# Casting a tile's weights one piece per matmul group instead of eight pieces per unit, in a hybrid decoder layer on Trainium2

## The reference

```python
u = rms_norm(h, norm_mix_g)
z_pool, z_q, z_k, z_v, z_gp, z_ga = split(u @ w_in)
pooled = multiscale_pool(z_pool)                    # windows 2/4/8/16, minus the token
mixed = einsum("blgc,gcd->blgd", pooled, pool_w)
y_pool = (mixed * pool_scale) @ w_pool_br
y_attn = sliding_window_attention(q, k, v, sinks, rel_bias) @ w_attn_br
merged = sigmoid(z_gp) * y_pool + sigmoid(z_ga) * y_attn
h = h + merged @ w_out
u2 = rms_norm(h, norm_mlp_g)
h = h + square(relu(u2 @ w_up)) @ w_down
h = rms_norm(h, norm_final_g)
```

## Time and profile before

| | us |
|---|---|
| median of 2 runs | 2581.69 (2487.75 and 2675.64) |
| the profiled execution | 2486.95 |
| its span on the slowest core, core 6 | 2485.4 |
| spans of the 8 cores | 2475.5 to 2485.4 |

### The profile page before, as it was taken

How to read it: one execution, slowest core, us unless ns; L and a number is a source line. 1 busy time by engine, 2 the same in 40 slices (tenths; PEclk the granted TensorE clock), 3 DMA queues, 4 the chain that set the end, 5 groups by cost and what they waited for, 6 DMA issues and landing times.

```text
span 2485.4 us, 28994 instructions; the slowest of 8 cores (2475.5 to 2485.4 us)
## 1 busy us (share of the span) xinstructions
PE 2139.6 (86%) x10254; PEld 976.0 (39%) x10432; DVE 607.6 (24%) x958; ACT 963.0 (39%) x1390; POOL 266.0 (11%) x262
## 2 busy tenths in 40 slices
PE   0575787698899989998799979998799988999798
PEld 0242233353444434443344524443344534444343
DVE  0112410224302250124302251024402242023401
ACT  5345554355212643155321543146321643124431
POOL 0000022000230004000040003100050002200050
PEclk9887998899999999999999999999999999999999
DMA  6876388741236303442145413453134502443132
GB/s 204 264 269 231 136 281 265 257 170 68 102 141 220 140 34 135 151 181 102 68 157 192 151 38 132 153 191 122 68 136 161 202 35 102 170 161 136 61 126 86
DMA packets 48990, 372.74 MB, mean 150 GB/s; under 512 B 5568, under 2 KB 5568, under 8 KB 32336
## 3 DMA queue, kind: packets, MB, share of 16 engines
q1 hardware_dynamic: 48848, 370.87, 42.1%
HBM read 321.04 MB, written 49.81 MB: 149 GB/s over the span
## 4 chain that ended last, share of the span: by engine, by line
PE 67%; DMA 11%; ACT 11%; issue 5%; DVE 4%; SPq 2%; ACTq 0%; DVEq 0%
PE ps L356 46%; PE ps L654 16%; ACT PT L529 4%; DMA stg<-w_dn 3%; DMA stg<-w_up 2%; PE ps L551 2%; DVE PT L531 2%; PE ps L553 1%; ACT tmpf L561 1%; SPq L259 1%; ACT sqj L316 1%; ACT wring L276 1%; PE ps L332 1%; DVE PT L534 1%; DMA stg<-w_q 1%
## 5 line engine op out<-in xcount | busy, mean ns | idle before, releaser
L637 POOL TENSOR_TENSOR arena<-tmpf 128x512 bf16<-128x512 f32 x256 | 265.2, 1041 | 2154.4 <-ACT tmpf L635 2154.3
L654 PE MATMUL ps<-wring,arena 128*128 128x512 bf16 x2008 | 444.4, 381 | 14.1 <-ACT tmpf L635 8.8
L356 PE MATMUL ps<-uT,wring 128*128 128x512 bf16 x1812 | 410.5, 385 | 19.4 <-ACT tmpf L635 11.6
L356 PE MATMUL ps<-Emp,wring 128*128 128x512 bf16 x1812 | 407.8, 384 | 8.1 <-DVE Emp L338 6.0
L654 PEld LDWEIGHTS ps<-wring,arena 128*128 128x128 bf16 x2048 | 201.0, 98 | 256.3 <-issue 16.9
L356 PEld LDWEIGHTS ps<-uT,wring 128*128 128x128 bf16 x1856 | 183.1, 99 | 238.7 <-issue 30.5
L356 PEld LDWEIGHTS ps<-Emp,wring 128*128 128x128 bf16 x1856 | 182.6, 99 | 225.3 <-issue 15.4
L635 ACT ACTIVATE tmpf<-ps 128x512 f32<-128x512 f32 x256 | 152.4, 597 | 299.4 <-PE ps L356 269.6
L529 ACT ACTIVATE PT<-ps 128x1536 bf16<-128x1536 f32 x128 | 184.7, 1443 | 154.4 <-PE ps L524 151.6
L356 PE MATMUL ps<-arena,wring 128*128 128x512 bf16 x616 | 144.4, 394 | 25.0 <-DVE arena L565 21.3
L553 PE MATMUL ps<-PT,cb 128*64 128x512 bf16 x384 | 145.2, 378 | 0.0
(11 more groups left out here) (82 smaller groups left out, 1775.0 us busy)
## 6 DMA issues: line engine op xcount, KB each, us to landing
wring<-w_up_bf SPq DMA_DIRECT2D x28, 2048.0 KB, 7.9
wring<-w_dn_bf SPq DMA_DIRECT2D x28, 2048.0 KB, 7.9
stg<-w_up SPq DMA_DIRECT2D x32, 512.0 KB, 7.3
stg<-w_dn SPq DMA_DIRECT2D x32, 512.0 KB, 8.3
wring<-w_pool_bf SPq DMA_DIRECT2D x7, 2048.0 KB, 7.8
wring<-w_q_bf SPq DMA_DIRECT2D x7, 2048.0 KB, 8.6
wring<-w_gp_bf SPq DMA_DIRECT2D x7, 2048.0 KB, 11.6
wring<-w_ga_bf SPq DMA_DIRECT2D x7, 2048.0 KB, 7.8
```

The lines of the kernel that those rows point to most:

```text
L356: ins = e.matmul(o, lhsT=pairs[kc][0], rhs=pairs[kc][1], start=(kc == 0), stop=(kc == nk - 1))
L637: P.op("pool", lambda e, c=c, ti=ti: e.tensor_tensor(out=arena[:, c, :], in0=tmpf[:, ti, :], in1=tmpf[:, ti, :], op=ALU.mult), reads=[("tm ...
L654: ins = e.matmul(bank(bk), lhsT=arena[:, j * 8 + kc, b * 128:(b + 1) * 128], rhs=w[:, kc, half * 512:(half + 1) * 512], start=(j == 0 and ...
```

## The change

The first tile's casts are no longer put into the queues all at once. `issue_unit` appends loads, casts and the store to lists. `pump()` takes the next cast (and a store that stands ahead of it) off the list and is called once ahead of each matmul group; `flush_upto(n)`, called by `need`, forces out whatever of unit n is left. `emit_loads()` keeps up to four loads ahead of the casts that have been taken off, across the border between units. The casts are also dealt out differently: two of three to ScalarE instead of three of four. Tiles 1 to 7 are written as before.

```diff
+    WQ = {"loads": [], "ops": [], "li": 0, "ci": 0, "groups_done": 0, "ngroups": 0}
...
+    def emit_loads():
+        while WQ["li"] < len(WQ["loads"]) and WQ["li"] < WQ["groups_done"] + NSTG:
+            WQ["loads"][WQ["li"]]()
+            WQ["li"] += 1
+
+    def pump_one():
+        n_, fn, closes, kind = WQ["ops"][WQ["ci"]]
+        WQ["ci"] += 1
+        fn()
+        if closes:
+            WQ["groups_done"] += 1
+        emit_loads()
+        return kind
+
+    def pump():
+        while WQ["ci"] < len(WQ["ops"]):
+            if pump_one() == "cast":
+                break
+
+    def flush_upto(n):
+        while WQ["ci"] < len(WQ["ops"]) and WQ["ops"][WQ["ci"]][0] <= n:
+            pump_one()
...
-                P.dma("sp", f"stg{s}",
+                WQ["loads"].append(lambda s=s, u=u, p=p, npc=npc, pc=pc: P.dma(
...
-                    eng = ("act", "act", "dve", "act")[cast_rr[0] % 4]
+                    eng = ("act", "dve", "act")[cast_rr[0] % 3]
...
-                    P.op(eng, fn, reads=[("stg", s), "scl"], writes=[("ws", slot, piece)])
+                    WQ["ops"].append((n, lambda eng=eng, fn=fn, s=s, slot=slot, piece=piece: P.op(
+                        eng, fn, reads=[("stg", s), "scl"], writes=[("ws", slot, piece)]), q == npc - 1, "cast"))
...
             W["issued"] += 1
+        flush_upto(n)
...
     def mm_group(b, nk, lhs_fn, rhs_fn, reads, out=None):
+        pump()
```

More of the change, by code:

```diff
@@ L237, in build_program @@
         si = (si + 1) % NSTG
-    stg_i = [si]
     W = {"issued": 0}
     cast_rr = [0]
+    WQ = {"loads": [], "ops": [], "li": 0, "ci": 0, "groups_done": 0, "ngroups": 0}
     def wslot_keys(slot):
         return [("ws", slot, p) for p in range(8)]
+    def emit_loads():
[17 more added lines that the diff above has]
+            pump_one()
     def issue_unit(n):
@@ L255, in issue_unit @@
                 npc = min(per_load, 8 - p)
-                s = stg_i[0]
-                stg_i[0] = (s + 1) % NSTG
-                P.dma("sp", f"stg{s}",
-                      lambda e, s=s, u=u, p=p, npc=npc, pc=pc: e.dma_start(out=stg[:, s, 0:npc * pc],
-                                                                           in_=wsrc[u][:, p * pc:(p + npc) * pc]),
-                      writes=[("stg", s)])
+                s = WQ["ngroups"] % NSTG
+                WQ["ngroups"] += 1
+                WQ["loads"].append(lambda s=s, u=u, p=p, npc=npc, pc=pc: P.dma(
+                    "sp", f"stg{s}",
+                    lambda e: e.dma_start(out=stg[:, s, 0:npc * pc], in_=wsrc[u][:, p * pc:(p + npc) * pc]),
+                    writes=[("stg", s)]))
                 for q in range(npc):
@@ L279, in issue_unit @@
                                                                                     scalar2=None, op0=ALU.mult)
-                    P.op(eng, fn, reads=[("stg", s), "scl"], writes=[("ws", slot, piece)])
+                    WQ["ops"].append((n, lambda eng=eng, fn=fn, s=s, slot=slot, piece=piece: P.op(
+                        eng, fn, reads=[("stg", s), "scl"], writes=[("ws", slot, piece)]), q == npc - 1, "cast"))
                 p += npc
             if nt > 1:
-                P.dma("sp", f"wst{u}", lambda e, u=u, slot=slot, sz=sz: e.dma_start(out=wbf[u], in_=wring[:, slot, 0:sz]),
-                      reads=wslot_keys(slot), writes=[("wbf", u)])
+                WQ["ops"].append((n, lambda u=u, slot=slot, sz=sz: P.dma(
+                    "sp", f"wst{u}", lambda e: e.dma_start(out=wbf[u], in_=wring[:, slot, 0:sz]),
+                    reads=wslot_keys(slot), writes=[("wbf", u)]), False, "store"))
+            emit_loads()
         else:
@@ L645, in build_program @@
                 assert W["issued"] >= NU
+                flush_upto(NU - 1)
                 load_x(1)
```

## The result

| | before | changed |
|---|---|---|
| median of all executions, us | 2488.87 (8) | 2459.45 (9) |
| ratio to before, with its 95% interval | | 0.9887 (0.9874 to 0.9900) |
| profiled execution, us | 2486.95 | 2459.09 |
| its span, us | 2485.4 | 2457.5 |
| spans of the 8 cores, us | 2475.5 to 2485.4 | 2443.3 to 2457.5 |

The change is 1.1% faster. The forecast was 2455 us, 1.3% less than before.

The account below looks back on a forecast made before the run. The first tile was taken to be bound by the weights' arrival, paced by the DMA queue. 31 + 8.3 - 8 = 31 us off 2486.95 us gave 2455 us, with a range from 2420 to 2488.

Parts of the forecast that it names:

- the forecast's own case: The forecast is for executions like the lower of the two runs shown before the change, 2487.75 us.
- (a): First tile, unit borders: closing the transfer holes at each unit's end wins 2.4 us at 13 borders, 31 us.
- (b): Ahead of attention: the last w_pb groups run while w_out is still coming in, which removes 8.3 us.
- (c): Behind attention and the RMSNorm: casts standing behind bank evictions add 3 us and 5 us, together 8 us.
- (d): End of the first tile: w_dn3's matmuls start at the last unit's store in both kernels, counted as nothing.
- rival C: First tile: TensorE working in small bites keeps the lower clock, 0.50, so the kernel is slower, 2534 us; chance 0.05.
- A: First tile: with the queue never empty, transfers run at 334 GB/s, 19 us per unit, giving 2425 us; chance 0.18.
- B: First tile: the rate is shared and other cores already use the holes; stays at 269 GB/s, 2487 us; chance 0.12.
- D: First tile: loads go out early, but casts behind evictions free their buffers no sooner, giving 2491 us; chance 0.07.
- T(8) near 206 and T(16) near 418: First tile: the stores of units 8 and 16 are issued near 206 us and near 418 us.
- windows below 200 GB/s at borders: First tile: no 4 us window at a unit border should be below 200 GB/s, except at w_pb.

Follow-up runs that it names:

- three of four: The changed kernel, but with three of four casts on ScalarE as before, instead of two of three: 2465.24 us, ratio to before 0.9900.
- ahead plus w_out: The kernel with only the loads ahead of the stores, with the w_out casts alone interleaved as well: 2454.34 us, ratio to before 0.9879.
- from w_up3 on: The kernel with loads ahead and w_out interleaved, with the casts of w_up3 and all w_dn units interleaved too: 2450.60 us, ratio to before 0.9870.

## Why the prediction was right

Its place, its mechanism and its sum hold: 2459.45 us against 2455, in the forecast's own case. Several terms are off with opposite signs, though, and that the sum is so close is in part luck. The terms, from the averages over 8 cores:

| term | forecast, us | measured, us | from |
|---|---|---|---|
| (a) holes before attention, 7 borders | -16.8 | -17.8 | T(8), before to changed |
| (b) the tail | -8.3 | -7.6 | item 1 behind T(8): 7.2 to -0.4 |
| (c) behind attention | +3 | +4.9 | item 1 to T(9): 55.9 to 60.8 |
| (a) w_up0 to w_up1 | -2.4 | -3.3 | T(9) to T(10): 23.0 to 19.7 |
| (c) behind the norm | +5 | +7.0 | T(10) to T(11): 23.8 to 30.8 |
| (a) five borders after it | -12 | -13.1 | T(11) to T(16): 115.8 to 102.7 |
| sum to T(16) | -31.5 | -29.9 | T(16): 445.9 to 416.0 |
| (d) end of the tile | 0 | +2.1 | T(16) to first output store: 8.3 to 10.4 |
| (d) later tiles | 0 | -2.9 | first output store to the end: 2025.4 to 2022.5 |
| whole sum | -31.5 | -30.7 | mean of the 8 spans: 2479.6 to 2448.9 |

(a) was worked out as 2.4 us per border from the bytes missing in a 4 us hole, and came out at 2.5 before attention and 2.6 after the norm. It wasn't that each hole closed: the 2 us up to a store carry 226 GB/s on the average, and 121 in the window shown. The rate behind it rose too: 353 GB/s in the ten microseconds from 384 on, beside 326 before. The experiment with only the loads ahead shows that this term alone carries the change: ratio 0.9894 without any interleaving.

(b) is confirmed twice, by putting it back (7.2 us at item 1) and by taking it alone (item 1 from 6.7 us behind T(8) to 0.3).

(c) was under-sized at both places, 4.9 for 3 and 7.0 for 5. I had worked out the eighth cast from the pace of the matmul groups, and it came later. (a) was under-sized by 3.0 us, so that the two errors nearly cancel in the table. The prediction put the whole interleaving at 8.3 - 8, near nothing, and for the whole kernel so it is: with the loads ahead in both, adding it changes the ratio from 0.9894 to 0.9887, within the intervals. But this too is a sum of opposite parts. At T(16) the kernel with only the loads ahead is 2.5 us sooner than the change (413.5 and 416.0), and its later tiles take 2.8 us longer (2025.3 and 2022.5). Without the loads ahead the interleaving costs 0.4%.

(d), nothing at the end of the tile, did not hold. Before, w_dn3's last matmul came 14.3 us behind T(16) on the average, in the change 16.4. The w_dn3 row of core 4, before and changed:

```profile
444.04 13.97 PE L654 MATMUL ps<-wring,arena 128*128 128x512 bf16 x64 [1.78 <-ACT wring L270]
410.42 16.73 PE L684 MATMUL ps<-wring,arena 128*128 128x512 bf16 x64 [7.41 <-ACT wring L293]
```

TensorE now waits 7.41 us for the last cast, and the first 4 us of the stage run at the lower clock:

```profile
444.04:448.04 4.00, 4.00 (x19) 1.85 (x20) 0.90 (x2) 0.00 (x0) 0.00 (x0) 1.00 0.94 385
410.42:414.42 4.00, 4.00 (x10) 1.43 (x11) 0.26 (x1) 0.00 (x0) 0.00 (x0) 0.50 0.94 328
```

It does 10 matmuls in them instead of 19. This comes near rival C's mechanism, for a part of one stage.

The later tiles, which I had expected to take the same time, take 2.9 us less, and the record shows with what this goes along. In the five traces of kernels with three of four casts on ScalarE (before, loads ahead only, three of four, ahead plus w_out, and from w_up3 on) the stretch from the first output store to the end takes 2025.3 to 2027.5 us. In the seven traces with two of three it takes 2021.3 to 2022.9, also where both kinds ran on one chip. The casts themselves are over by then, and the tiles are written alike; why they differ stays open. (The trace of the first run with only the loads ahead, of a 2821.44 us execution, is not counted.)

The rivals. A (334 GB/s, 2425 us) fell: with the DMA engines busy 95% of the time the rate is 304 GB/s, so little is left to gain with this mix of loads and stores. Its premise was also read too narrowly. The 334 GB/s of rows 9 are the best 10 us of the first tile, not of the trace; in a later tile the kernel before reaches more, and the changed kernel has 392 GB/s from 430 to 440 us. So the prediction's remark that the best 10 us stay below the figure that it cites does not hold. Core 6, before:

```profile
500.00:510.00 10.00, 9.95 (x47) 4.51 (x46) 0.69 (x1) 2.98 (x5) 0.00 (x0) 1.00 0.90 360
```

A's 23 us after attention should also have been 449.6 - 423 = 26.6, which changes nothing here.

B (holes already used by other cores) fell: the windows of all 8 cores show 301 to 309 GB/s from 62 to 200 us where they showed 263 to 274, so that closing all cores' holes raised all rates. C fell as a whole with the clock of 0.97 from 312 to 410 us; it was 0.88 on core 6 in the same window before. In small it is real: in w_dn3, and in attention once casts were put there (clock 0.83). D fell at T(8), though its observation is right that interleaved casts free the staging buffers later. That this keeps the rest of the holes open is argued from the order of the queues, not tried.

Of the signs I had named, T(8) near 206 and T(16) near 418 came out at 206.1 and 425.3 on the slowest core, 202.4 and 416.0 over all of them. The full units from w_up3 on take 20.5 us, not 21.7, and T(11) comes 30.8 us behind T(10), not 28. One sign failed: windows below 200 GB/s at borders are still there (170 at 379 to 383 us). It was a poor sign, since the kernel with the interleaving alone shows 167 and 151 in such windows with its holes open.

## What to carry to other kernels

Where a store waits in the same in-order DMA queue as the next loads, put those loads ahead of it as far as staging buffers come free. The hole between them is worth its missing bytes at the rate beside it, and here that gave 31.2 us for 34.2 measured. Interleaving casts with the work that empties banks paid in these traces only where that work was otherwise held up in the chain that ends last (here ahead of attention, and 1.7 us at w_dn); where data already waits in staging, it should be taken in one go. A moment inside the kernel that comes sooner is not yet time won: follow it to the first output store and to the end, since here 9.6 us at T(16) became 2.3 us of the mean span.

## What I had not expected of the hardware

Eight casts added to attention (about 8 us together) made that stretch 7.6 us longer on the average of the cores, and 10 on core 0 (45.4 to 55.5 us), though ScalarE was busy for only about two thirds of it. Idle time inside a chain of small hand-offs was not free: at a clock of 0.97 the casts still cost 6.2 to 6.4 us. The rest goes along with a lower granted clock, down to 0.83, in a stretch where it had been 1.00 on all cores.

The windows of 2 us up to a unit's store carry 6 and 16 GB/s in the two kernels whose loads stand behind the store, and 226 and 259 in the two whose loads stand ahead of it; over a whole MLP stretch the slowest cores have 274 and 241 GB/s in the first two and 291 and 294 in the others. The transfers' rate here was set by the order of the queue.

The later tiles, in which no instruction is written differently, differ by some 3 to 5 us between kernels that deal out the first tile's casts differently, and repeat within 0.3 us in the two traces of the changed kernel (2022.5 and 2022.2).
